# Projections moved under two scans: q, k and v beside a state-space scan, an output projection in the last phases of a time-mix scan

## What is computed

```python
# first block, layer 0 (h is the normed and modulated input, 256 x 1024)
z, xbc, dt_raw, q, k, v = split(h @ w_in)          # widths 2048, 3072, 32, 3072, 1024, 1024
xbc = silu(causal_depthwise_conv(xbc))             # 4 taps -> xs (2048), B (512), C (512)
y = ssd_chunked(xs, softplus(dt_raw + bias), A, B, C) + d_skip * xs   # 4 groups, 2 chunks of 128
y = rms_norm(y * silu(z), g)
att = dilated_attention(q, k, v, rel_table)
mix = concat([y, att]) @ w_out

# second block, layer 0 (RWKV time mix over ctx and x, 512 tokens, both directions)
r, k, v, g = projections of four shifted mixtures  # each 1024 x 1024
o = two_way_state_scan(r, k, v, decay, rate)       # 16 heads of 64, here 8 pairs of heads
o = (group_norm(o) + bonus) * silu(g)
d = o @ w_out                                      # 1024 x 1024; the projection that moves
ctx, x = ctx + g_c * d[:256], x + g_x * d[256:]
```

## Time and profile before

| | |
|---|---|
| median of three runs | 2572.72 us |
| profiled execution, its time | 2568.52 us |
| its span | 2566.8 us |
| TensorE busy | 2276.0 us, 89% of the span |
| VectorE, ScalarE, GpSimd busy | 38%, 20%, 12% |
| TensorE's mean granted clock | 0.937 |
| DMA | 359.75 MB, 140 GB/s |

### The profile page before, as it was taken

How to read it: one execution, slowest core, us unless ns; L and a number is a source line. 1 busy time by engine, 2 the same in 40 slices (tenths; PEclk the granted TensorE clock), 3 DMA queues, 4 the chain that set the end, 5 groups by cost and what they waited for, 6 DMA issues and landing times. The chain is left out here.

```text
span 2566.8 us, 40218 instructions
## 1 busy us (share of the span) xinstructions
PE 2276.0 (89%) x16920; PEld 1682.1 (66%) x16920; DVE 974.0 (38%) x2194; ACT 522.6 (20%) x926; POOL 319.0 (12%) x558
## 2 busy tenths in 40 slices
PE   2999966789999999999998688999998899879998
PEld 1888855578788886688873345565566667446546
DVE  3124436430343057277316244424424531120253
ACT  1011012320100010200013334333333422011142
POOL 0000000000000030000003544333432011000000
PEclk9999987799999999999999789998999889889989
DMA  7455520414686421187504665545544241313100
GB/s 298 184 225 218 197 100 0 81 23 161 273 303 232 177 104 50 66 332 297 207 1 163 215 171 161 148 124 139 137 122 110 49 112 44 150 51 117 47 1 17
DMA packets 126267, 359.75 MB, mean 140 GB/s; under 512 B 78600, under 2 KB 87048, under 8 KB 108304
## 3 DMA queue, kind: packets, MB, share of 16 engines
q1 hardware_dynamic: 93776, 213.05, 24.2%
q0 software_dynamic: 31744, 143.16, 16.5%
q10 hardware_dynamic: 576, 1.05, 0.1%
HBM read 340.36 MB, written 16.85 MB: 139 GB/s over the span
## 5 line engine op out<-in xcount | busy, mean ns | idle before, releaser
L271 PE MATMUL bank<-h,ring 128*128 128x256 f32 x2944 | 638.2, 380 | 4.8 <-DVEq L975 3.3
L271 PEld LDWEIGHTS bank<-h,ring 128*128 128x128 f32 x2944 | 560.3, 190 | 84.7 <-DVEq L975 4.9
L1755 PE MATMUL bank<-rw_feed 128*128 128x512 f32 x464 | 255.4, 658 | 22.3 <-DMA rw_feed<-in_rkvg 22.2
L185 PE MATMUL bank<-con 128*128 128x512 f32 x290 | 142.7, 644 | 91.9 <-PEq L257 57.6
L1571 POOL DMA_DIRECT2D rw_feed<-rwkv_mixes x232 | 124.5, 537 | 501.2 <-PE bank L1755 492.0
L185 PEld LDWEIGHTS bank<-con 128*128 128x128 f32 x290 | 58.0, 204 | 160.9 <-issue 160.3
L885 PE MATMUL bank<-ffn_hidden,ring 128*128 128x256 f32 x704 | 152.4, 379 | 3.4 <-PEq L911 3.4
L2056 DVE TENSOR_TENSOR rw_u<-bank,rw_lam 128x128 f32<-128x128 f32 x120 | 35.0, 291 | 301.8 <-PE bank L1702 298.3
L885 PEld LDWEIGHTS bank<-ffn_hidden,ring 128*128 128x128 f32 x704 | 133.6, 190 | 22.2 <-issue 4.1
L1755 PEld LDWEIGHTS bank<-rw_feed 128*128 128x128 f32 x464 | 79.3, 200 | 88.4 <-issue 45.7
L1572 POOL DMA_DIRECT2D rw_feed<-in_rkvg x232 | 124.2, 535 | 10.1 <-issue 10.1
(11 more groups left out here) (394 smaller groups left out, 3304.2 us busy)
## 6 DMA issues: line engine op xcount, KB each, us to landing
ring<-in_stream SPq DMA_DIRECT2D x81, 2048.0 KB, 8.1
rw_feed<-rwkv_mixes POOLq DMA_DIRECT2D x232, 256.0 KB, 3.0
next_w<-in_mod_stream POOLq DMA_DIRECT2D x24, 2048.0 KB, 10.4
ctx<-in_mod_rest POOLq DMA_DIRECT2D x16, 1024.0 KB, 7.2
rw_feed<-in_rkvg POOLq DMA_DIRECT2D x232, 64.0 KB, 3.2
rwkv_mixes<-mixed SPq DMA_DIRECT2D x8, 1024.0 KB, 3.9
y<-bias_table SPq DMA_DIRECT2D x48, 128.0 KB, 4.8
rw_at<-rw_at_kept SPq DMA_DIRECT2D x16, 256.0 KB, 5.7
```

The source lines that it names most:

```text
L185: pe.matmul(k.psum[bank][:], const(k, "ident"), k.con[:, 0:512], start=True, stop=True)
L271: mm = pe.matmul(out, ring_tile(k, n, kt, i * P), rhs[kt], start=start and kt == kts[0], stop=stop and kt == kts[-1])
L1755: pe.matmul(k.psum[PROJ], feed[:, g % FEED, 512:], feed[:, g % FEED, 0:512], start=(kt == 0), stop=(kt == KT - 1)).then_inc(eaten, 1)
```

## The change

In the first block, `stage_hyin` keeps ten slots: the columns for XBC first, then z. Its iterations take `mod_rest` halves by HALVES: two in iteration 0, one in each of 1 to 6, three in 7, three in 8, two in 9; and two pairs of the convolution in each of 1 to 6. `stage_dt`, `stage_ssd` and `stage_ssm_gate` with its norm become one block, `stage_ssm`, written out without loops, in which PE also makes the other 40 tiles (q, k, v) in PSUM banks 6 and 7 with ScalarE storing them in pairs. The decay rows, which had banks 4 to 7, alternate in banks 4 and 5, with waits on `masked` and `rowed` for it. silu(z) moves into this block on ScalarE.

In the second block, the output weights no longer come through slots but as eight tiles `wout[0..7]` of 512 KB into dead places of the scan's buffers: six by GpSimd's queue in phase 5, two by SP's. `stage_rwkv_out` is gone. Its 64 products become `out` items and its sums `add` items in phases 6, 7 and 8, accumulated in three parts per output tile (n 0 to 3, 4 to 6, 7), through bank 7, the last part through banks 0 to 7. The gate's products of pairs 6 and 7 move from 0.04 to 0.9 to 0.04 to 0.3. The scan's buffers in the ring are ordered anew, and SP loads two slots of the next stage at the start of phase 7 and two behind the chain.

```diff
+NFIRST = 10
-    PHASES = ((0, 2, True, False), (2, 2, True, True), (4, 1, False, True))
+    HALVES = [(0, 2)] + [(n + 1, n + 2) for n in range(1, 7)] + [(8, 11), (11, 14), (14, 16)]
...
+            for n in range(NFIRST):
+                for half in range(*HALVES[n]):
+                    half_slot(half)
+                for p in turns(n):
+                    convolve(p)
+                dve.wait_ge(k.slot_used, first + n + 1)
+                nc.vector.tensor_copy(y[:, place(n):place(n) + 2, :],
+                                      k.psum[2 * (n % 2)].rearrange("p (i t) -> p i t", i=2)).then_inc(stored_dve, 1)
...
+            def project(t):
+
+                n, pair = first + t // 4, t // 2
+                if t % 4 == 0:
+                    wait_slot(k, pe, n)
+                if t % 2 == 0 and pair >= 2:
+                    pe.wait_ge(stored, pair - 1)
+                for kt in range(KT):
+                    mm = pe.matmul(k.psum[6 + pair % 2][:, (t % 2) * T:(t % 2 + 1) * T],
+                                   ring_tile(k, n, kt, (t % 4) * P), h[:, kt, :], start=(kt == 0), stop=(kt == KT - 1))
...
+            for t in range(4):
+                project(t)
+            pe.wait_ge(dt_step, 11)
...
+            for g in range(4):
+                t = 4 + 5 * g
+                turn(g)
+                rows(g, 0)
+                rows(g, 1)
+                project(t)
+                rows(g, 2)
+                rows(g, 3)
+                project(t + 1)
+                states(g)
+                project(t + 2)
+                outputs(g, 0)
+                project(t + 3)
+                outputs(g, 1)
+                project(t + 4)
+            for g in range(4):
+                project(24 + g)
+                pe.wait_ge(squared, g + 1)
+                for i in range(4):
+                    mm = pe.matmul(k.psum[3][:, 0:T], const(k, "ones"), squares[:, g % 2, T * i:T * i + T],
+                                   start=(g + i == 0), stop=(g + i == 6))
+                mm.then_inc(sq_summed, 1)
+            for t in range(28, NT):
+                project(t)
...
+FIRST_PAIRS, NEXT_PAIRS, LAST_PAIR = (0, 1, 2, 3), (4, 5, 6), (7,)
+def scan_out(m, pairs):
+
+    return [("out", n, m, pairs) for n in pairs] + [("add", pairs[-1], m, pairs)]
+
+
+def scan_outs(i):
+
+    lists = {KT - 2: [(0.34, 1, range(0, 5), FIRST_PAIRS)],
+             KT - 1: [(0.32, 0.58, range(5, KT), FIRST_PAIRS), (0.58, 1, range(0, 4), NEXT_PAIRS)],
+             KT: [(0, 0.24, range(4, KT), NEXT_PAIRS), (0.4, 1, range(KT), LAST_PAIR)]}.get(i, [])
...
-                            (0.04, 0.3 if i + 4 < KT else 0.9, has(i, scan_project(i, 3))),
+                            (0.04, 0.9 if KT - 4 <= i < KT - 2 else 0.3, has(i, scan_project(i, 3))),
+                            *scan_outs(i),
...
+            sp.wait_ge(gr_up, 4 * (KT - 1))
+            sp.wait_ge(o_out, 64)
+            sp.dma_start(early, o_kept).then_inc(late_landed, 16)
+            for n in range(6, KT):
+                sp.dma_start(wout[n], a["rwout"][n]).then_inc(late_landed, 16)
             sp.wait_ge(step_up, (NCK + 1) * (KT - 2))
             for dst, src in zip((k.x, k.ctx), x_kept):
                 sp.dma_start(dst[:].rearrange("p a t -> p (a t)"), src.ap()).then_inc(back, 16)
-            sp.wait_ge(gr_up, 28)
-            sp.wait_ge(o_out, 64)
-            sp.dma_start(early, o_kept).then_inc(back, 16)
-            sp.wait_ge(back, 48)
+            sp.wait_ge(step_up, (NCK + 1) * (KT - 1))
+            sp.wait_ge(gr_up, 4 * KT)
+            for n in range(2):
+                sp.dma_start(k.ring[:, (first + n) % RING, :], k.stream[first + n]).then_inc(
+                    k.slot_landed[(first + n) % RING], 16)
...
+                if n == KT - 2 and j == 3 and g % KT == 0:
+                    pool.wait_ge(el_done, 2 * KT)
+                    pool.wait_ge(bon_down, KT)
+                    for m in range(6):
+                        pool.dma_start(wout[m], a["rwout"][m]).then_inc(wout_landed, 16)
...
+            def wide_free(item):
+
+                at = wide.index(item)
+                if at and wide[at - 1][0] == "add":
+                    pe.wait_ge(add_done, 2 * adds.index(wide[at - 1]) + 2)
+                elif at:
+                    m, l = wide[at - 1][1:]
+                    if l == 3:
+                        pe.wait_ge(sg_done, m + 1)
...
+                elif kind == "add":
+                    m, pairs = item[2:]
+                    at = adds.index(item)
+                    dve.wait_ge(out_up, at + 1)
+                    dve.wait_ge(back, 32)
...
+                    for dst, cols, c in ((k.ctx, slice(0, T), True), (k.x, slice(T, 2 * T), False)):
+                        v.scalar_tensor_tensor(dst[:, m, :], src[:, cols], mod2(k, 0, GT, c)[:, m:m + 1], dst[:, m, :],
+                                               ALU.mult, ALU.add).then_inc(add_done, 1)
...
-def stage_rwkv_out(nc, k, o):
```

More of the change, by code:

```diff
@@ L301, in stage_hyin, with place, turns @@
         block = ctx.enter_context(nc.Block())
-        def over_phases(eng, one, between=None):
-            for t0, turns, mod, conv in PHASES:
-                for t in range(turns):
-                    for j in range(RING):
-                        one(t, j, t0, mod, conv)
-                if between is not None and t0 == 0:
-                    between()
+        def place(n):
+            return ST_XS + 4 * n if n < 6 else ST_Z + 4 * (n - 6)
+        def turns(n):
+            return (2 * n - 2, 2 * n - 1) if 1 <= n <= 6 else ()
         @block.sync
@@ new lines, in rows @@
+            def rows(g, b):
+                bt, ct, xs, hv = group(g)
+                c, half = b // 2, b % 2
+                if b >= 2:
+                    pe.wait_ge(masked, 4 * g + b - 1)
+                elif g:
+                    pe.wait_ge(masked, 4 * (g - 1) + b + 3)
+                    pe.wait_ge(rowed, 2 * (g - 1) + b + 1)
+                for i in range(4):
+                    col = hv[:, DA, c, half * 4 + i:half * 4 + i + 1].to_broadcast([P, P])
+                    mm = pe.matmul(k.psum[4 + b % 2][:, i * P:(i + 1) * P], col, const(k, "tri"), start=True, stop=True)
+                mm.then_inc(rows_up, 1)
@@ new lines, in _ @@
+            dve.wait_ge(sq_summed, 4)
+            nc.vector.tensor_scalar(rstd, k.psum[3][:, 0:T], 1.0 / DI, EPS, ALU.mult, ALU.add).then_inc(normed, 1)
+            dve.wait_ge(rooted, 1)
+            nc.vector.reciprocal(rstd, rstd).then_inc(normed, 1)
+            dve.wait_ge(normed, 2)
+            for i in range(16):
+                nc.vector.scalar_tensor_tensor(y[:, ST_XS + i, :], y[:, ST_XS + i, :], row(k, "ssmg", i), rstd, ALU.mult,
+                                               ALU.mult)
@@ L667, in stage_ssm_gate, with store @@
-def stage_ssm_gate(nc, k, y):
-    with ExitStack() as ctx:
-        half_done = ctx.enter_context(nc.semaphore("gate_done"))
-        block = ctx.enter_context(nc.Block())
-        @block.vector
-        def _(dve):
-            for lo, hi in ((0, 4), (4, 8), (8, 12), (12, 16)):
-                nc.vector.tensor_tensor(y[:, ST_XS + lo:ST_XS + hi, :], y[:, ST_XS + lo:ST_XS + hi, :],
-                                        y[:, lo:hi, :], ALU.mult)
-    stage_norm(nc, k, y[:, ST_XS:ST_XS + 16, :], 16, T, row(k, "ssmg", 0, 16), None,
-               y[:, ST_XS:ST_XS + 16, :], "ssm")
+            def store(t):
+                if t % 2 == 0:
+                    return
+                pair = t // 2
+                if pair % 2 == 0:
+                    act.wait_ge(half_up, pair // 2 + 1)
+                else:
+                    act.wait_ge(k.slot_used, first + pair // 2 + 1)
+                at = ST_Q + 2 * pair
+                dst = y[:, at:at + 2, :] if at < ST_K else y[:, at:at + 2, ::-1]
+                nc.scalar.copy(dst, k.psum[6 + pair % 2].rearrange("p (i t) -> p i t", i=2)).then_inc(stored, 1)
@@ new lines, in _ @@
+            for g in range(4):
+                t = 4 + 5 * g
+                decay(g, 0)
+                decay(g, 1)
+                store(t)
+                decay(g, 2)
+                decay(g, 3)
+                store(t + 1)
+                act.wait_ge(states_up, g + 1)
+                if g:
+                    act.wait_ge(y_up, 2 * g)
+                nc.scalar.copy(state[:], k.psum[3][:]).then_inc(state_down, 1)
+                for i in range(2, 5):
+                    store(t + i)
@@ new lines, in _ @@
+            for g in range(4):
+                store(24 + g)
+                act.wait_ge(gated, g + 1)
+                if g == 0:
+                    act.wait_ge(y_up, 8)
+                if g >= 2:
+                    act.wait_ge(sq_summed, g - 1)
+                nc.scalar.activation(squares[:, g % 2, :], y[:, ST_XS + 4 * g:ST_XS + 4 * g + 4, :].rearrange(
+                    "p i t -> p (i t)"), ACT.Square).then_inc(squared, 1)
+            act.wait_ge(normed, 1)
```

(7 more changed lines are left out.)

483 lines of the change are left out of this document (233 added, 250 removed).

## The result

The changed kernel takes 0.9873 of the time before (95% interval 0.9853 to 0.9893): 2542.08 us, the median of three runs (2536.80 to 2546.03), beside 2573.81 of the kernel before on the same chip, 31.7 us less by the medians and 32.7 by the ratio. A fourth run, 3102.24 us at a mean granted clock of 0.717, was in a slower state and is left out of all these figures. The forecast was 31 us off the profiled 2568.5, and 2541 for the median. The profiled execution after takes 2542.08 us, span 2540.4, so between the two profiled executions the gain is 26.4 us.

The account below looks back on a forecast made before the run. TensorE, busy 89% of the span, was taken as the bound. Gains of 15 us (Part A) and 16 (Part B) took the profiled 2568.5 to 2537.5; with the median 4.2 higher, 2541.7, rounded 2541, range 2518 to 2563.

Parts of the forecast that it names:

- The modulation tail: End of input stage: TensorE stands after slot 9 while modulation halves pass through one buffer, 28 us lost (19 to 36).
- R1: Rival, input stage: modulation halves keep up, so TensorE does not stand; kernel 2513 us; chance 0.08.
- The bias write: End of input stage: the bias table's write, holding the end 7.4 us behind a slot load, is hidden under TensorE's standing.
- Groups: State-space scan: four groups, each 11.9 us of scan work plus five tiles of 17.4, 29.3 each, 117 in all.
- R3: Rival, state-space scan: interleaved scan bound by latency, 4.2 us a group uncovered, 17 in all; kernel 2557; chance 0.08.
- The bias wait: Start of attention: VectorE's first step waits longer for bias loads behind a 2 MB load, 5 us (0 to 6).
- Part A: Last ten projection slots (q, k, v) moved inside the state-space scan's stage: 15 us gained (3 to 31).
- In the chain: Long scan, phases 6 and 7: 44 output products placed there add 43 us (36 to 54), almost nothing hidden.
- Behind the chain: Long scan's chain end to last sum: 26 us instead of 84.8, a gain of 59 (54 to 63).
- Part B: Output projection moved inside the long scan: 16 us gained (0 to 27).
- R2: Rival, long scan: waits stretch each moved product's step 0.36 us more, the output projection's gain falls to 0; 2557; chance 0.12.
- R4: Rival, new state-space stage: short mixed tiles keep TensorE's clock low; 100 us of it give 2591; chance 0.05.

Follow-up runs that it names:

- four buffers: Changed kernel with four buffers instead of one for the modulation halves, each load waiting for the half four before it: 0.979 of the kernel before, 2519.7 us.
- held slots: Changed kernel with the slot loads freed by input-stage slots 7, 8 and 9 issued only after all 16 modulation halves are used: 0.9878 of the kernel before.
- when alone: Kernel before with only the projection inside the state-space scan (Part A): ratio 0.9947; with only the output projection inside the long scan (Part B): 0.9948.

## Why the prediction was right, and where it was not

The sum was 31 us; 31.7 to 32.7 came by the runs, 26.4 between the profiled executions. The main mechanisms hold: the standing behind the single buffer, the scan that takes the tiles in, the chain that hides nothing, the boundary that goes. That the total came so close is in part luck: misses of 3 to 10 us in single terms cancelled. (The forecast of 2541.7 rounds to 2542, not 2541.) Term by term, in the prediction's order:

- *The modulation tail*, 28 us lost (19 to 36): the mechanism was right in its place, its releaser and its form; it cost 36.8, just outside its bounds. The step that was mis-sized is the landing of 6.4 us, taken between 5.1 and 7.5: it left out that a half can start at the same time as a slot load; then 10.5. The bounds were taken from a stage in which that never happened. R1 is refuted: the tail is there, and only with four buffers does the next stage start 28.7 us earlier.
- *The bias write is hidden in that*: right, with 9.4 us on SP's queue under the 36.8; and it came out from under as soon as the cover was gone (9.1 us with four buffers, 16.4 seen with held slots).
- *Four tiles and dt*, 16 + 5.5: 15.6 + 4.9. *Groups*, 29.3 each: 26.5. This step was wrong: it took 11.9 busy us from a row whose clock was 0.81, as if that were the work; at full clock it is 9.1. Four groups took 107.5 and not 117.2, which happened to make up for the tail's 9. R3 is refuted: no wait of TensorE's is left in a group, and without the tiles the 16.6 us come back.
- *Squares and the last tiles*, 24 and 41.8: 24.5 and 41.6. *Attention at 448.7*: 446.75. *The bias wait*, 5 us (0 to 6): 3.4 in VectorE's start, 0.4 in the end of the stage.
- Part A to the output stage: 21.2 gained where 15 were forecast. Part A to the end: 13.7 (9 to 19) when alone. The difference is the longer stretch at the long scan's start, in part waits on loads, which no step had, since I asked what is late next only up to attention.
- *In the chain*, 43 us (36 to 54): 44.4 to the chain's end, 1.01 a product. But it is made of other things than I said. Phase 6 needed 12.7 us for 20 products, where 0.92 each make 18.4; phase 7 to the chain's end 31.7 for 24, where they make 22.1. The clock of phase 6, 0.83 in rows 1 and without a term, gave back about 6 us; the 3.5 expected in phase 7 did not come, as the thin stretch at 2161 to 2175 brought 12 us at the lower level. The slots that start with phase 7, priced at 0 to 3, cost 3.5 in feeds and part of that clock, and with them held back phase 7 is 5.5 shorter. The gate cost 2.5 where 3 stood. The six weights in phase 5, bounded by 0 to 4, cost nothing in the kernel after; the 2.8 us on the solved matrices appear only where no product fills the wait.
- *Behind the chain*: the sum of the tail was 26 from the chain's end and 30.0 came. The reading ended at +20.1, not +18: its four waits on sums took 3.5 us, not 2.4, and TensorE stood 2.35 for the last o, where I had all idle time filled. The last eight products and their sum then took 9.8 us, not 8, as the clock had fallen (0.63 over the first 4.6 us).
- Part B: 10.5 gained in the trace, 13.4 by the ratio when alone; 16 forecast, within 0 to 27. R2, 0, is refuted; R4 too: the 195 us from 251.66 to attention run at a mean clock of 0.98, where 0.77 stood in the scan. The Trainium skill ("TensorE: Matmul & The Clock Gate", section What's actually happening) said that activity releases the throttled state; the trace agrees for that stage, and the thin stretch at 2161 to 2175 in phase 7, which TensorE left at 0.50, agrees from the other side.

The Trainium skill ("DMA: Bandwidth & Descriptors", section Issuing engines are not separate DMA queues) was used to say that halves and slots interleave. The trace agrees, 10.5 beside 5.0. I took the size from the range observed before, 5.1 to 7.5, and the rule gave no reason to stop there.

## What to carry to other kernels

Placing work between the pieces of a serial computation pays where the engine is idle or at a low clock in that stretch: read both there first (49 of 71 us busy at 0.77 gave 26.8 us in four groups, 90 of 92 gave nothing), and where there is nothing to gain take the simple order. When a transfer with one buffer loses the work that covered it, price its landing with every other load in flight at once, or give it buffers that lie unused at that time; and put small writes that a stage's end waits for ahead of the large loads on their queue. A busy time read at a low clock isn't work: convert it before it goes into a sum.

## What the runs showed of the hardware

Two loads on different queues that start together finish together: 1 MB beside 2 MB landed in 10.5 us and the 2 MB in 9.7, where 1 MB alone took 5.0 and 2 MB, with only the small write behind it, 7.8. A 72 KB write behind one 2 MB load took 7.4 us from issue to landing, behind three of them 17.6. A serial ring of TensorE and VectorE (16.1 to 16.6 us a group) didn't move when TensorE's mean clock went from 0.81 to 0.90 and 0.96.
